# The front of a hybrid encoder layer: first projection on x times the norm's weight, the root applied afterwards, loads reissued

## What is computed

```
h = rms_norm(x, g)                      # x * rsqrt(mean(x*x) + eps) * g
a_val, a_gate, u, g_conv, g_ssm = split(h @ w_in)          # 768, 768, 256, 1024, 1024 columns
v = depthwise_conv_31(a_val * sigmoid(a_gate)) + conv_b    # causal, 31 taps
y_conv = silu(layer_norm(v)) @ w_conv_out
y_ssm  = s5(u)                          # B u, complex scan over 256 steps, C state, gelu, glu
x += (sigmoid(g_conv) * y_conv + sigmoid(g_ssm) * y_ssm) @ w_out
x += moe(rms_norm(x))                   # 32 experts, top 4, 12 MB of weights an expert
out = rms_norm(x)
```

## Time and profile before

| | |
|---|---|
| runs | 1098.1, 1096.65, 1096.41 us; median 1096.65 |
| profiled execution | 1099.46 us, its span 1097.7 us (1.76 us lie around the span) |
| PE busy | 1057.2 us, 96% of the span |
| DVE, ACT, POOL busy | 299.5, 148.4, 81.0 us |
| DMA | 430.06 MB read from HBM, 393 GB/s over the span |
| chain that ended last | PE 71%, DMA 26%, ACT 1%, DVE 1% |

### The profile page before, as it was taken

The page is one execution under the profiler, slowest core; times in us unless marked ns, Lnnn a source line. Parts: engine busy times, 40 slices in busy tenths (PEclk is TensorE's granted clock), DMA queues, the critical chain, the costliest instruction groups (busy, mean ns, idle before and its releaser), DMA issues.

```text
span 1097.7 us, 12142 instructions
## 1 busy us (share of the span) xinstructions
PE 1057.2 (96%) x4957; PEld 455.9 (42%) x4958; DVE 299.5 (27%) x686; ACT 148.4 (14%) x268; POOL 81.0 (7%) x155
## 2 busy tenths in 40 slices
PE   7999999999999999999999999999999999989996
PEld 6888876333333333333333333333323333323332
DVE  5999843311111111111111111111111011111112
ACT  3011403101010101111010000000000000000012
POOL 2986110000000000000000000000000000000000
PEclk9999999999999999999999999999999999999999
DMA  7947795899999999999999999999999999999995
GB/s 240 272 122 301 296 355 229 350 402 429 429 435 430 431 436 426 435 431 431 436 426 435 432 428 434 426 435 432 431 435 427 435 432 430 435 427 426 428 422 232
DMA packets 43657, 431.52 MB, mean 393 GB/s; under 512 B 6775, under 2 KB 22445, under 8 KB 25484
## 3 DMA queue, kind: packets, MB, share of 16 engines
q1 hardware_dynamic: 43356, 430.60, 94.0%
q10 hardware_dynamic: 272, 0.52, 0.1%
HBM read 430.06 MB, written 1.05 MB: 393 GB/s over the span
## 4 chain that ended last, share of the span: by engine, by line
PE 71%; DMA 26%; ACT 1%; DVE 1%; another core or an unknown queue 1%; issue 0%; SPq 0%; DVEq 0%
PE bank L1617 30%; DMA ring<-w_gate_up 22%; PE bank L1629 14%; PE bank L1362 10%; PE bank L1643 4%; PE bank L1555 3%; DMA ring<-w_down 3%; PE bank L1469 2%; PE bank L1497 2%; ACT area L759 1%; PE bank L1583 1%; PE bank L1608 1%; PE bank L1511 1%; PE bank L1588 1%; PE bank L1457 1%
## 5 line engine op out<-in xcount | busy, mean ns | idle before, releaser
L1617 PE MATMUL bank<-ring,area 128*64 128x512 f32 x2048 | 455.9, 601 | 17.6 <-DMA ring<-w_gate_up 17.6
L1617 PEld LDWEIGHTS bank<-ring,area 128*64 128x64 f32 x2048 | 149.6, 139 | 306.5 <-issue 272.0
L1629 PE MATMUL bank<-ring,area 128*64 128x512 f32 x1024 | 229.3, 599 | 5.9 <-ACT area L759 2.8
L1192 DVE TENSOR_SCALAR area<-bank 128x512 f32<-128x512 f32 x32 | 22.1, 692 | 670.7 <-PE bank L1617 670.7
L1629 PEld LDWEIGHTS bank<-ring,area 128*64 128x64 f32 x1024 | 72.0, 137 | 142.9 <-issue 133.3
L1362 PE MATMUL bank<-area,ring 128*128 128x256 f32 x480 | 109.0, 388 | 1.4 <-DMA ring<-w_in 1.4
L1362 PEld LDWEIGHTS bank<-area,ring 128*128 128x128 f32 x480 | 92.5, 194 | 16.2 <-DMA ring<-w_in 1.7
L765 ACT ACTIVATE area<-area 128x512 f32<-128x512 f32 x32 | 20.1, 630 | 484.6 <-DVE area L1192 484.6
L971 DVE SCALAR_TENSOR_TENSOR bank<-ring,spread,bank 128x256 f32<-128x256 f32 x174 | 71.5, 483 | 0.6
L1643 PE MATMUL bank<-area,spT 64*128 64x512 f32 x248 | 61.6, 615 | 0.7 <-ACT area L762 0.7
L1555 PE MATMUL bank<-rows,pick 128*64 128x512 f32 x256 | 62.2, 605 | 0.0
(11 more groups left out here) (263 smaller groups left out, 494.4 us busy)
## 6 DMA issues: line engine op xcount, KB each, us to landing
ring<-w_gate_up SPq DMA_DIRECT2D x48, 4096.0 KB, 46.7
ring<-w_down SPq DMA_DIRECT2D x25, 4096.0 KB, 44.2
ring<-w_gate_up SPq DMA_DIRECT2D x19, 2048.0 KB, 18.2
ring<-w_gate_up SPq DMA_DIRECT2D x26, 1024.0 KB, 9.3
ring<-w_down SPq DMA_DIRECT2D x18, 1024.0 KB, 12.6
ring<-w_in SPq DMA_DIRECT2D x15, 1024.0 KB, 8.2
ring<-w_down SPq DMA_DIRECT2D x5, 2048.0 KB, 12.9
ring<-w_conv_out SPq DMA_DIRECT2D x1, 3072.0 KB, 12.7
```

What stands on the lines that cost most here:

```text
L1192: return v.tensor_scalar(gc, bank[4][:, :], 7.0, None, ALU.min)
L1617: last = mm(bank[4 + b][64 * h:64 * h + 64, :], heT[:, k % 4, k // 4 * 64:k // 4 * 64 + 64], fours(w, b, h), start=False, stop=(k == KD - 1))
L1629: last = mm(bank[b][64 * h:64 * h + 64, :], src[:, k % 4, k // 4 * 64:k // 4 * 64 + 64], w[:, k % 2, h * 512:h * 512 + 512], start=(k == 0 ...
```

## The change

It does these things.

1. PE runs ten products of the identity with itself (START_WARM) before it turns x. The norm's weight g comes with x (third load of SP) and is turned between the two tiles of x.
2. x^T times g (hraw) is made at once, chunks 0 to 3 by DVE, 4 to 7 by ACT. The first half of chunk 0 multiplies hraw (`first_half`), with the spreading of the root and the turning of the parameters after its fourth product; DVE multiplies its result by the root (z_half) before the Sigmoid. hT, for all that follows, is hraw times the root.
3. SP issues conv_w and w_in first (chunk 0 in two parts), ssm_b and ssm_c behind chunk 5; the nine other parameter loads go by ACT's queue, ahead of its first instruction.
4. The taps are turned after the first half of chunk 0; C and B are turned together after chunk 5, and ACT copies them behind its takes of chunks 2, 4 and 5. B's six products with the discretized factors move from DVE to POOL (raw_b), which does them with the masking of C (raw_c) ahead of the sixth level of its tables. DVE does the rest of the discretization after its first ten taps.
5. In the convolution's norm the first half of chunk 14 goes ahead of the channel sum, and the first bias_part goes behind the scaling. Two table loads of ACT are asked for earlier by small dummy activations.
6. The refill of expert 28 uses the loop's semaphores and sizes (4, 4, 4), which is what its entry in END had.

```diff
+START_WARM = 10
...
+            sp.dma_start(par_rows[0:8, :], norm_mix_g[0].rearrange("(k p) -> k p", p=128)).then_inc(x_in[1], 16)
...
-            load_win(0)
-            load_win(1)
             sp.dma_start(tap_rows, conv_w[0]).then_inc(tap_in, 16)
+            win0, win0_v = grid(at(0, CH), KD, 256), win_v[:, :, ORDER[0] * 256:ORDER[0] * 256 + 256]
+            sp.dma_start(win0[:, 0:4, :], win0_v[:, 0:4, :]).then_inc(win_in[0], 16)
+            sp.dma_start(win0[:, 4:8, :], win0_v[:, 4:8, :]).then_inc(win0_late, 16)
+            for c in range(1, WRING):
+                load_win(c)
...
-            refill_end(E - 4, 0, PER)
+            refill(E - 6, 0, MIDDLE)
...
+                if k == 5:
+                    raw_c()
+                    raw_b()
...
+            act.dma_start(log_steps, ssm_log_step[0].rearrange("(t g) -> t g", g=2)).then_inc(par_in, 16)
+            for src, r0 in ((ssm_a_re, 8), (ssm_a_im, 16)):
+                act.dma_start(par_rows[r0:r0 + ST, :], src[0].rearrange("(t g) p -> t (g p)", g=2)).then_inc(par_in, 16)
+            for src, r0, n in ((norm_ffn_g, 24, 8), (conv_b, 40, 6), (conv_ln_g, 46, 6), (conv_ln_b, 52, 6), (ssm_d, 58, 2),
+                               (b_ssm_glu, 60, 2)):
+                act.dma_start(par_rows[r0:r0 + n, :], src[0].rearrange("(k p) -> k p", p=128)).then_inc(par_in, 16)
             act.wait_ge(consts, 1)
             s.activation(neg_top, ident[:, 0:2], ACT.Sqrt)
...
             act.wait_ge(var_x, 1)
             s.activation(rstd, ss, ACT.Sqrt).then_inc(std_x, 1)
-            act.wait_ge(params_pe, 1)
-            s.activation(par[:, :], bank[7][:, 0:54], ACT.Copy).then_inc(params_sb, 1)
+            act.wait_ge(raw_dve, 1)
+            for k in range(4, KD):
+                act.wait_ge(xT_pe, k // 2 + 2)
+                s.activation(hraw[:, k, :], bank[k // 2][:, k % 2 * T:k % 2 * T + T], ACT.Copy, scale=g_early[:, k:k + 1])\
+                    .then_inc(raw_act, 1)
             act.wait_ge(spread_pe, 1)
             s.activation(rstd_all, bank[6][:, 0:T], ACT.Copy).then_inc(rstd_sb, 1)
+            act.wait_ge(params_pe, 1)
+            s.activation(par[:, :], bank[7][:, 0:62], ACT.Copy).then_inc(params_sb, 1)
+            s.activation(neg_top, ident[:, 0:2], ACT.Sigmoid)
+            act.wait_ge(params_pe, 2)
+            s.activation(late[:, 62:62 + KC * W], bank[7][:, 62:62 + KC * W], ACT.Copy).then_inc(params_sb, 1)
+            act.wait_ge(z_half, 1)
+            s.activation(sig_a[:, 0, :], sig_a[:, 0, :], ACT.Sigmoid).then_inc(half_sig, 1)
...
+            take(2)
+            take(4)
+            take(5)
             act.wait_ge(rawT_pe, 1)
             s.activation(cT, grid(bank[0][:, :], 2, 2, 128), ACT.Copy).then_inc(rawT_sb, 1)
             s.activation(c_neg, grid(bank[0][:, :], 2, 2, 128)[:, :, 0, :], ACT.Copy, scale=-1.0).then_inc(rawT_sb, 1)
-            take(2)
             act.wait_ge(rawT_pe, 2)
             s.activation(bT, grid(bank[1][:, :], 2, 2, 128), ACT.Copy).then_inc(rawT_sb, 1)
-            take(4)
-            take(5)
...
+            def raw_rows(b):
+                dve.wait_ge(xT_pe, b + 2)
+                v.tensor_tensor(hraw[:, 2 * b:2 * b + 2, :], grid(bank[b][:, :], 2, T),
+                                g_early[:, 2 * b:2 * b + 2].unsqueeze(2).to_broadcast([128, 2, T]), ALU.mult).then_inc(raw_dve, 1)
+            dve.wait_ge(xT_pe, 1)
+            v.tensor_copy(g_early, bank[7][:, 0:8]).then_inc(raw_dve, 1)
+            dve.wait_ge(raw_dve, 1)
+            raw_rows(0)
             dve.wait_ge(x_sq, TT)
             var_of_sum(D).then_inc(var_x, 1)
+            raw_rows(1)
             dve.wait_ge(std_x, 1)
             link(v.reciprocal(rstd, rstd))
             dve.wait_ge(consts, 1)
             for t in range(TT):
                 v.tensor_scalar(diag[:, t, :], ident[:, :], rstd[:, t:t + 1], None, ALU.mult).then_inc(diag_ready, 1)
-            dve.wait_ge(params_sb, 1)
+            dve.wait_ge(raw_dve, 3)
             dve.wait_ge(rstd_sb, 1)
             for k in range(KD):
-                v.scalar_tensor_tensor(hT[:, k, :], bank[k // 2][:, k % 2 * T:k % 2 * T + T], p_g[:, k:k + 1],
-                                       rstd_all, ALU.mult, ALU.mult).then_inc(hT_ready, 1)
+                if k >= 4:
+                    dve.wait_ge(raw_act, k - 3)
+                v.tensor_tensor(hT[:, k, :], hraw[:, k, :], rstd_all, ALU.mult).then_inc(hT_ready, 1)
+                if k == 3:
+                    dve.wait_ge(half_pe, 1)
+                    v.tensor_tensor(sig_a[:, 0, :], half_bank[0][0], rstd_all, ALU.mult).then_inc(z_half, 1)
+            dve.wait_ge(params_sb, 1)
...
-            taps_of(order[:scanning])
+            taps_of(order[:LEAD])
+            discretize()
+            taps_of(order[LEAD:scanning])
...
-            dve.wait_ge(bias_in, 48)
-            bias_part(96)
...
+            dve.wait_ge(bias_in, 48)
+            bias_part(96)
             bias_part(64)
...
+            for _ in range(START_WARM):
+                mm(bank[6][:, 256:384], ident[:, :], ident[:, :], start=True, stop=True)
             for t in range(TT):
-                pe.wait_ge(x_in[t], 16)
+                pe.wait_ge(x_in[t], 16 * (t + 1))
+                if t == 1:
+                    tr(bank[7][:, 0:8], par_rows[0:8, :], ident[0:8, 0:8]).then_inc(xT_pe, 1)
                 for k in range(KD):
...
+                    last = tr(bank[k // 2][:, (k % 2) * T + t * 128:(k % 2) * T + t * 128 + 128],
+                              x_sb[:, t, k * 128:k * 128 + 128], ident[:, :])
+                    if t == 1 and k % 2:
+                        last.then_inc(xT_pe, 1)
...
+            def first_half():
+                w = grid(at(0, CH), KD, 256)
+                for k in range(KD):
+                    if k == 0:
+                        pe.wait_ge(win_in[0], 16)
+                    if k == 4:
+                        pe.wait_ge(win0_late, 16)
+                    if k in (0, 2):
+                        pe.wait_ge(raw_dve, 2 + k // 2)
+                    if k >= 4:
+                        pe.wait_ge(raw_act, k - 3)
+                    last = mm(half_bank[0][0], w[:, k, 0:128], hraw[:, k, :], start=(k == 0), stop=(k == KD - 1))
+                    if k == 3:
+                        spread_rstd()
+                last.then_inc(half_pe, 1)
+            def spread_rstd():
+                pe.wait_ge(ones_ready, 1)
+                for t in range(TT):
+                    pe.wait_ge(diag_ready, t + 1)
+                    last = mm(bank[6][:, t * 128:t * 128 + 128], ones, diag[:, t, :], start=True, stop=True)
+                last.then_inc(spread_pe, 1)
+                pe.wait_ge(par_in, 16 * 9)
+                pe.wait_ge(ls_rows, 1)
+                tr(bank[7][:, 0:62], par_rows[:, :], ident[0:62, 0:62]).then_inc(params_pe, 1)
...
-            project(0, (0,))
-            project(1, (0,))
+            first_half()
             pe.wait_ge(tap_in, 16)
             pe.wait_ge(params_sb, 1)
             for k in range(KC):
                 last = tr(bank[7][:, 62 + k * W:62 + k * W + W], tap_rows[:, k * 128:k * 128 + 128], ident[0:W, 0:W])
             last.then_inc(params_pe, 1)
+            project(1, (0,))
             project(0, (1,))
             project(1, (1,))
-            pe.wait_ge(raw_ready, 1)
             pe.wait_ge(params_sb, 2)
-            raw_transpose(craw, 0)
             project(2)
             project(3)
+            project(4)
+            project(5)
+            pe.wait_ge(raw_ready, 1)
+            raw_transpose(craw, 0)
             pe.wait_ge(raw_ready, 2)
             raw_transpose(braw, 1)
-            project(4)
-            project(5)
+            freed(4)
             pe.wait_ge(rawT_sb, 3)
-            freed(4)
             bu_pair(0)
...
+            project(14, (0,))
             pe.wait_ge(conv_done, KC + 1)
             pe.wait_ge(bu_sb, ST)
             mm(bank[0][:, 0:T], ones, conv[:, KC - 1, :], start=True, stop=False)
             mm(bank[0][:, 0:T], ones, conv_sum, start=False, stop=True).then_inc(mean_pe, 1)
-            project(14, (0,))
...
-            for e in range(E - 4, E - 2):
-                expert(e, e % 2, e)
+            expert(E - 4, 0, [(E // 2 - 2) * 16 + n for n in later(0)])
+            expert(E - 3, 1, E - 3)
```

More of the change, by code:

```diff
@@ L104, in build @@
         squares = grid(at(17, CH), TT, D)
+        hraw = grid(at(14, CH), KD, T)
         gateC = grid(at(17, CH), KD, T)
@@ L177, in build @@
         late = spread[:, :, :, :].rearrange("p t d s -> p (t d s)")
-        par = late[:, 0:54]
-        gain_k = late[:, 54:62]
+        par = late[:, 0:62]
+        gain_k = late[:, 24:32]
         taps = grid(late[:, 62:62 + KC * W], KC, W)
@@ L235, in build @@
         x_sq = sem("x_sq")
+        xT_pe = sem("xT_pe")
+        raw_dve = sem("raw_dve")
+        raw_act = sem("raw_act")
+        z_half = sem("z_half")
+        win0_late = sem("win0_late")
         var_x = sem("var_x")
```

(32 more changed lines are left out.)

104 lines of the change are left out of this document (39 added, 65 removed).

## The result

The changed kernel takes 1101.98 us in the median of 7 runs (1098.07 to 1102.55), the kernel before 1096.41 (1095.26 to 1098.1): a ratio of 1.0046, 95% interval 1.0036 to 1.0055 (the quotient of the two medians is 1.0051). It is **slower by 5.6 us**, 0.5%, and 3.8 us above the top of the predicted range. Its profiled execution took 1101.62 us (span 1099.7).

What follows compares the result with a forecast made beforehand. The experts' weight stream runs at the DMA engines' full rate, so PE's front shifts the end. Terms -1.9 - 2.9 + 0.6 + 1.1 + 0.15 = -2.95, say -2.9, from median 1096.65 give 1093.8 us; range 1092.3 to 1098.2.

Steps and rivals of the forecast that it cites:

- The surplus of the first 32 passes goes: -2.9 us: PE's first passes: 10.04 us where the next 32 take 7.17; warm-up removes the half-speed surplus, -2.9 us.
- it would land at 8.4 ... Cost nothing; if it were late, up to 1: w_in's first half megabyte, issued at about 2.8 us, lands before PE's first product at 8.75; cost 0, at most 1.
- The clock rises and falls again: Rival: PE's clock falls between warm-up and first product, or rises late; 1.7 us lost, 1095.5 us; chance 0.23.
- The warm-up does not bring the clock up: Rival: warm-up only delays x, PE's surplus of 2.9 stays; +0.8 us, 1097.4 us; chance 0.25.
- The rule of transposes: PE's clock at the front: transposes do not count as work that raises it; cited as speaking against the change.
- Turning x, -1.9: Front, PE's transposes of x at the upper clock: first product at 8.75 instead of 10.64 us, -1.9 us.
- Spread and parameters inside the first half, +0.6 (0.5 to 1.2): Formerly in the wait for w_in, now on PE's path in chunk 0's first half: +0.6 us, bounds 0.5 and 1.2.
- C and B, +1.1 (0.9 to 1.3): Behind chunk 5, PE does their transposes and waits for ACT's copies: +1.1 us, bounds 0.9 and 1.3.
- The convolution's norm, up to +0.15: At the channel sum, squares are summed about when PE arrives for the state space part's product: up to +0.15 us.
- ACT's squares, nothing: Squares of x end near 8 instead of 6.4 us behind nine loads; bound 0.5 us, taken as nothing.
- A microsecond of the front is therefore a microsecond of the end: Before expert 0: whatever the front gains or loses shifts the whole stream of expert weights, hence the end, equally.
- The stream of weights takes no notice: Rival: transfers already full before expert 0, end stays at 1096.7 us; chance 0.10, shared with an unseen wait.

Runs made afterwards that it cites:

- the second profile: Kernel before, unchanged, profiled again; that execution took 1096.14 us, first 32 passes 7.17 us.
- the first profile of before: Kernel before, unchanged, the profile the prediction read; that execution took 1099.46 us, first 32 passes 10.04 us.
- the third profile of before: Kernel before, unchanged, profiled once more; that execution took 1096.93 us, first 32 passes 8.83 us.

## Why the prediction was wrong

Against an execution of before at its median time (the second profile, 1096.14 us, expert 0 at 196.36) the changed kernel's expert 0 is 5.83 us later (202.19), and its median is 5.6 us higher. Point by point:

- **"The surplus of the first 32 passes goes: -2.9 us"** failed first. The other two profiles had 0 and 1.7 us of it to remove. The prediction saw that its profile was 2.8 us above the median and explained it away with "the front's steps are the same in both". They were not: expert 0 began 2.4 us later than in the profile of 1096.14 us. Without this term its sum is 0, and the forecast would have been "no change".
- **"it would land at 8.4 ... Cost nothing; if it were late, up to 1"** (the term of w_in) failed too, and this is the step that made the result slower: 5.6 us where the sum had nothing. It priced the load by its bytes and its place, and not the load put ahead of it, whose 31 rows run one at a time. The wait cost 3.1 us, and the clock that fell in it 2.5 (the changed kernel against the version with four loads). Before, conv_w ran in the same way (31 packets in a row, 12.7 to 16.6 us), behind both chunks of w_in and with 4 us to spare ahead of its transposes at 20.6; the packet records were there, but none of the rows that the prediction used shows them.
- The rival "**The clock rises and falls again**" came true in its mechanism, but was priced for a "short wait" of PE: 1.7 us where it was 2.5. "**The warm-up does not bring the clock up**" is refuted: in the six profiles with it the clock rose at 4.4 to 7.7 us, in four of them (4.4 to 5.1) before the first transpose. The eight profiles without it, in which the transposes come first, differ among themselves: the clock rose during them at 7.1, 7.2, 7.8 and 8.0 us in four, once at 8.5 in the small products right behind them and once at 10.2 in the first products with w_in, but in the first profile of before and in that of `START_WARM = 0` alone only at 16.5 and 16.4. The rule of transposes that the prediction cited from the Trainium skill ("TensorE: Matmul & The Clock Gate", Part 4, PE-mode transpose) fits the last two and not the four; the measurement decides. That transposes often do the warm-up's work would explain why it is worth nothing in the median (1095.67 against 1095.89); that is argued, not shown.
- **Turning x, -1.9**: right in size, by luck. With conv_w in four loads the first product is at 8.93 instead of 10.77, -1.84, but it waits 1.15 us for w_in; DVE's first product with g had ended at 7.92. The identity's passes took 0.22 us each at the lower level (20 from 1.57 to 6.00 us in the changed kernel), not 0.253, and the clock rose before their end, so x was ready sooner than 8.75; w_in, behind three more issues, landed later than 8.4. The two errors cancel; with conv_w's loads behind w_in the first product is at 8.32.
- **Spread and parameters inside the first half, +0.6 (0.5 to 1.2)**: from the first product to the end of 32 passes it is 4.98 + 16 x 0.222 = 8.53 us with the change, and 7.59 before (second profile): +0.94, inside the bounds.
- **C and B, +1.1 (0.9 to 1.3)**: right. The first B u is at 54.19 against 53.97, so 0.22 later after having been 0.9 ahead: +1.12; and moving them gave 1.2 back.
- **The convolution's norm, up to +0.15**: right in effect. Expert 0 is again 0.22 later (196.58 against 196.36), so between the first B u and there the change costs nothing in sum.
- **ACT's squares, nothing**: right. They end at 7.7 us, and DVE takes the variance between its products with g.
- **"A microsecond of the front is therefore a microsecond of the end"**: right, and the rival "The stream of weights takes no notice" is refuted. In the 14 profiles expert 0 starts between 194.78 and 203.79 us, and the time less that start is 897.9 to 899.8 us, but for the two with a half-speed stretch at expert 0's down products (900.7 and 901.2).
- **The range**: its upper end is called the case without a rise "with 0.5" more, which is 1097.9 and not 1098.2. The result is outside both.

The corrected sum, -1.84 + 0.94 + 1.12 = +0.22, and with conv_w's 5.6 us +5.8, is the 5.83 measured. Its terms are read from three single profiles (the changed kernel, the version with four loads, the second one of before), so tenths in it are not to be trusted: against the third profile of before the changed kernel's expert 0 is 4.7 us later.

## What to carry to other kernels

Before a term is built on a profile's odd stretch, ask whether that execution is typical: when its time is above the median by as much as the stretch is worth, the stretch is probably the reason, and a second profile of the unchanged kernel is the cheapest experiment there is. A load's cost to those behind it isn't its bytes: look in the packet records whether its rows run side by side or one at a time (31 rows did here), and split it (16 + 8 + 4 + 3 here) or put it where nobody waits. A wait of PE right behind a warm-up can cost nearly twice: here 3.1 us for itself and 2.5 for the clock.

## What was not expected of the hardware

- 93 KB in 31 packets of 3 KB took 5.1 us, where x's two loads of 512 KB took 3.2 us from issue to landing in the median; in loads of 16, 8, 4 and 3 rows 1.3 us.
- The moment of the clock's rise varies between executions of the same instructions: 16.5, 8.5 and 7.2 us in the kernel before, 7.1 and 4.5 in the changed one, with PE starting at the same time to 0.1 us. What decides it was not tried.
- Twice in 14 profiles the clock fell for 3.4 us behind the short operations ahead of expert 0's down products (at 217.9 and 222.2 us), 1.7 us each time; the same instructions kept it in the other twelve.
